# One 512-column matmul for the high and low halves of the features in the FFN up-projection, with the modulation spread over five FFNs

## The chip, the cores and the metric

The kernel runs on one core of one Trainium2 chip. The metric is device time in microseconds. Three runs of the kernel before took 2191.59, 2196.65 and 2203.82 us; the median is 2196.65 us.

## The reference, cut to what matters

Two models run one after the other on a sequence of 256 tokens of width 1024, each with two layers, all in float32. The layers of the first hold a mixer of several attentions and an FFN with a convolution; the layers of the second hold an FFN, a token mixer and a second FFN. That makes six FFNs, numbered here in the order in which they run: FFN 1 and 2 in the layers of the first model, FFN 3 and 4 in the first layer of the second model, FFN 5 and 6 in its last layer.

```python
def conv_glu_ffn(h, w_up, conv_w, conv_b, w_down):          # FFN 1 and 2
    a, u = jnp.split(h @ w_up, 2, axis=-1)                  # w_up: 1024 x 5632
    a = causal depthwise convolution of a, 3 taps, + conv_b
    return (jax.nn.silu(a) * u) @ w_down                    # w_down: 2816 x 1024

def swiglu(h, w13, w2):                                     # FFN 3 to 6
    a, b = jnp.split(h @ w13, 2, axis=-1)
    return (jax.nn.silu(a) * b) @ w2

# second model, layer l
mod = (jax.nn.silu(c) @ ada_w[l] + ada_b[l]).reshape(b_, 3, 3, 1024)
y = swiglu(modulate(x, mod[:, 0, 0], mod[:, 0, 1]), ffn_w13[l, 0], ffn_w2[l, 0])
x = layer_norm(ALPHA * x + 0.5 * (1 + mod[:, 0, 2]) * y, ...)
y = token_mixer(modulate(x, mod[:, 1, 0], mod[:, 1, 1]), ...)
x = layer_norm(ALPHA * x + (1 + mod[:, 1, 2]) * y, ...)
y = swiglu(modulate(x, mod[:, 2, 0], mod[:, 2, 1]), ffn_w13[l, 1], ffn_w2[l, 1])
```

`mod` does not depend on the tokens: it is a product of one vector with a matrix of 1024 by 9216 for each of the two layers.

## The kernel before, in words

**The split.** Each float32 operand of a projection is split into a high part that TensorE multiplies in its fast float32 format and a low part, the rest. A product is the sum of three: high by high, high by low, low by high (`products`, L610 to L612). The weights come in chunks of 1 MB (128 partitions by 2048 numbers) through a ring of three slots. For each chunk ScalarE writes `w_hi` (`hi`, L1101) and VectorE then writes `w_lo` as `raw` minus `w_hi` (`lo`, L1487). A transfer into a slot of `raw` is issued by SyncE once `lo` of the chunk before it in that slot is done.

**An FFN.** It has 22 tiles of 128 hidden features, each with an `a` half and a `u` half, and 33 chunks: 22 for up, 11 for down. TensorE does tile 0, then in turn two up tiles and one down chunk (`turn`), and at the end one up tile and one down chunk. An up tile is 16 steps (8 tiles of the width for each half), and each step is three matmuls that move 256 columns. A down chunk is 24 matmuls that move 512 columns. In FFN 3 to 6 the gate of the residual is spread over the partitions by TensorE behind up tile 0 (`gate_on_all`) and copied by ScalarE (L1305).

**Behind an up tile.** Its result lies in one PSUM bank of two (`UP`). ScalarE waits for the tile and makes the convolution's first tap (L1128) or `silu` (L1131), then `hi` of a later chunk, and, in FFN 1 and 2, `silu` (L1135) behind the other two taps. VectorE makes those two taps (L1514, L1517), `lo` of a later chunk, and then `h` = `silu(a)` times `u` (L1521), still reading PSUM. ScalarE writes `hid_hi` (L1137), VectorE `hid_lo` (L1523). Up tile f+2 waits for `h` of tile f, since it writes the same bank; the down chunk waits for `hid_lo`.

**The modulation.** It is done on VectorE beside the FFNs (`ada`, `modulation`, L1481): 72 chunks of 1 MB from `wm`, two operations for each, 144 in all. Before, FFN 1, 2, 3 and 5 carry 18 chunks each. `silu(c)` comes first (`silu_c`, L1095, on ScalarE) and the first three chunks, six operations, stand on VectorE ahead of `post(0, ...)`; the rest is placed behind `hid_lo` of certain tiles in `turn`.

**Layers.** On every engine a hardware loop (`Fori`) runs over the two layers of each model. At a layer's end PE, ACT and DVE drain, GpSimd clears the semaphores and raises `layer_go`, and all begin the next layer. The order of work on each engine is that of the code, and no planner changes it.

## Time and profile before

| | |
|---|---|
| span of the profiled execution | 2196.9 us |
| its own time | no other than the span is recorded |
| median of three runs | 2196.65 us |
| TensorE matmul busy | 1971.7 us (90%), 13906 matmuls |
| TensorE weight loads busy | 1839.9 us (84%) |
| VectorE busy | 1405.2 us (64%) |
| ScalarE busy | 964.2 us (44%) |
| GpSimd busy | 135.9 us (6%) |
| mean granted TensorE clock | 0.944 |
| moved by DMA | 373.22 MB, mean 170 GB/s |

Matmuls are pipelined, and the duration of one in a row is longer than the distance to the next one's start; the distance is what counts. PE is TensorE, DVE is VectorE, ACT is ScalarE, POOL is GpSimd, SP is SyncE, whose time is that of issuing transfers. The granted clock 1.00 is 2.4 GHz and 0.50 is 1.2 GHz.

### The profile page before, as it was taken

The page shows a single profiled execution, that of the slowest core. Times are in us where ns is not written, and L with a number is a line of the kernel's source. Part 1 is how long each engine was busy: PE and PEld are TensorE (multiplying, and loading weights), DVE is VectorE, ACT ScalarE, POOL GpSimd, SP SyncE. Part 2 cuts the span into 40 slices and gives each one's busy share as a digit, 9 for nine tenths or more (in the row PEclk, how much of TensorE's full clock was granted, in tenths as well). Part 3 has the DMA queues.
Part 4 walks back from the last instruction along what each step waited for, and adds up shares of the span by engine and source line. Part 5 has one row for each costly group of instructions (what it writes and reads, how often), then busy time and mean ns, then how long its engine had stood idle before and what let it go on. Part 6 is the DMA issues. An engine that isn't in the chain of part 4 may idle for free.

```text
span 2196.9 us, 36223 instructions
## 1 busy us (share of the span) xinstructions
PE 1971.7 (90%) x13906; PEld 1839.9 (84%) x13906; DVE 1405.2 (64%) x2155; ACT 964.2 (44%) x1479; POOL 135.9 (6%) x202
## 2 busy tenths in 40 slices
PE   7978999798899969997998979987998898888997
PEld 7868999787899959996888969976997787887996
DVE  4486777448677867667647564556667754756545
ACT  4454444445544444344553334324443545424342
POOL 0000000000000000002005110000000200501000
PEclk9999999989999989998999889997999899988999
DMA  7116676311667667762410235537874251024552
GB/s 270 44 54 267 250 293 246 144 44 58 254 251 293 247 254 273 271 230 83 167 58 1 95 136 178 186 134 267 301 268 176 90 180 39 1 96 140 185 191 77
DMA packets 54109, 373.22 MB, mean 170 GB/s; under 512 B 5984, under 2 KB 6880, under 8 KB 10848
## 3 DMA queue, kind: packets, MB, share of 16 engines
q1 hardware_dynamic: 51392, 361.45, 45.6%
q0 software_dynamic: 2016, 9.07, 1.1%
q8 instruction: 82, 1.34, 0.2%
q10 hardware_dynamic: 576, 0.99, 0.1%
q14 instruction: 43, 0.35, 0.1%
HBM read 370.45 MB, written 1.05 MB: 169 GB/s over the span
## 4 chain that ended last, share of the span: by engine, by line
PE 79%; DVE 13%; ACT 5%; issue 3%; DMA 0%; DVEq 0%; ACTq 0%; POOLq 0%; SPq 0%
PE bank L610 17%; PE bank L611 17%; PE bank L612 17%; PE bank L673 5%; PE bank L674 5%; PE bank L675 5%; PE bank L1030 1%; PE bank L1039 1%; DVE hT_lo L1850 1%; DVE w_lo L1487 1%; PE bank L1038 1%; DVE scratch L1481 1%; PE bank L626 1%; PE bank L649 1%; ACT w_hi L1101 1%
## 5 line engine op out<-in xcount | busy, mean ns | idle before, releaser
L610 PE MATMUL bank<-hT_hi,w_hi 128*128 128x256 f32 x2432 | 703.9, 289 | 56.3 <-DVE hT_lo L1850 29.1
L1487 DVE TENSOR_TENSOR w_lo<-raw,w_hi 128x2048 fp32r<-128x2048 f32 (+2 forms) x270 | 609.0, 2257 | 142.7 <-ACT w_hi L1101 142.3
L611 PE MATMUL bank<-hT_lo,w_hi 128*128 128x256 f32 x2432 | 697.0, 287 | 0.0
L612 PE MATMUL bank<-hT_hi,w_lo 128*128 128x256 f32 x2432 | 696.5, 286 | 0.0
L1101 ACT ACTIVATE w_hi<-raw 128x2048 fp32r<-128x2048 f32 (+2 forms) x270 | 509.0, 1887 | 193.9 <-PE bank L675 119.8
L610 PEld LDWEIGHTS bank<-hT_hi,w_hi 128*128 128x128 f32 x2432 | 473.9, 195 | 66.3 <-DVE hT_lo L1850 31.4
L611 PEld LDWEIGHTS bank<-hT_lo,w_hi 128*128 128x128 f32 x2432 | 473.7, 195 | 4.9 <-issue 2.0
L612 PEld LDWEIGHTS bank<-hT_hi,w_lo 128*128 128x128 f32 x2432 | 473.3, 195 | 0.7
L610 PE MATMUL bank<-w_hi,hT_hi 128*128 128x256 f32 (+2 forms) x800 | 233.0, 291 | 2.0 <-DVE hT_lo L1504 2.0
L611 PE MATMUL bank<-w_lo,hT_hi 128*128 128x256 f32 (+2 forms) x800 | 231.0, 289 | 0.0
L612 PE MATMUL bank<-w_hi,hT_lo 128*128 128x256 f32 (+2 forms) x800 | 230.8, 289 | 0.0
L673 PE MATMUL bank<-w_hi,hid_hi 128*128 128x512 f32 x528 | 207.0, 392 | 8.4 <-DVE hid_lo L1523 8.4
L674 PE MATMUL bank<-w_lo,hid_hi 128*128 128x512 f32 x528 | 206.3, 391 | 0.0
L675 PE MATMUL bank<-w_hi,hid_lo 128*128 128x512 f32 x528 | 205.4, 389 | 0.0
L1481 DVE SCALAR_TENSOR_TENSOR scratch<-scratch 128x1024 f32<-128x1024 f32 x144 | 171.1, 1219 | 12.0 <-ACT scratch L1095 12.0
L610 PEld LDWEIGHTS bank<-w_hi,hT_hi 128*128 128x128 f32 x800 | 159.4, 199 | 4.2 <-issue 4.1
L1131 ACT ACTIVATE scratch<-bank 128x256 f32<-128x256 f32 x88 | 33.8, 384 | 293.9 <-PE bank L612 293.6
L611 PEld LDWEIGHTS bank<-w_lo,hT_hi 128*128 128x128 f32 x800 | 159.4, 199 | 0.0
L612 PEld LDWEIGHTS bank<-w_hi,hT_lo 128*128 128x128 f32 x800 | 159.2, 199 | 0.0
L1523 DVE TENSOR_TENSOR hid_lo<-scratch,hid_hi 128x256 fp32r<-128x256 f32 x132 | 56.2, 425 | 158.5 <-ACT hid_hi L1137 158.5
L673 PEld LDWEIGHTS bank<-w_hi,hid_hi 128*128 128x128 f32 x528 | 99.4, 188 | 29.8 <-DVE hid_lo L1523 11.0
L1521 DVE TENSOR_TENSOR scratch<-scratch,bank 128x256 f32<-128x256 f32 x132 | 55.2, 418 | 107.2 <-ACT scratch L1131 106.2
(352 smaller groups left out, 2375.4 us busy)
## 6 DMA issues: line engine op xcount, KB each, us to landing
raw<-in_wb SPq DMA_DIRECT2D x168, 1024.0 KB, 5.0
raw<-in_wa SPq DMA_DIRECT2D x96, 1024.0 KB, 4.8
scratch<-in_wm SPq DMA_DIRECT2D x72, 1024.0 KB, 6.6
lnw<-in_ln_g POOLq DMA_DIRECT2D x6, 512.0 KB, 4.1
lnw<-in_ln_b POOLq DMA_DIRECT2D x6, 512.0 KB, 5.4
cst<-in_const POOLq DMA_DIRECT2D x1, 2205.0 KB, 9.8
raw<-in_wa SPq DMA_DIRECT2D x4, 512.0 KB, 3.5
scratch<-in_c SPq DMA_DIRECT2D x4, 512.0 KB, 4.3
```

What stands on the lines that cost most here:

```text
L610: nc.tensor.matmul(out, ah, bh, start=(i == 0), stop=False)
L611: nc.tensor.matmul(out, ah, bl, start=False, stop=False)
L612: last = nc.tensor.matmul(out, al, bh, start=False, stop=(i == n - 1))
L673: nc.tensor.matmul(out, ah, bh, start=first and k2 == 0, stop=False, skip_group_check=True)
L674: nc.tensor.matmul(out, ah, bl, start=False, stop=False, skip_group_check=True)
L675: last = nc.tensor.matmul(out, al, bh, start=False, stop=last_one and k2 == 1, skip_group_check=True)
L1101: nc.scalar.activation(w_hi[:, slot, 0:width], raw[:, raw_slot, 0:width], ACT.Copy).then_inc(hi_done, 1)
L1131: nc.scalar.activation(sg[:, f2, :], UP[f2][:, 0:SEQ], ACT.Silu).then_inc(N["sg"], 1)
L1481: return nc.vector.scalar_tensor_tensor(out=w, in0=w, scalar=1.0, in1=cb, op0=ALU.mult, op1=ALU.mult, accum_out=column)
L1487: nc.vector.tensor_tensor(w_lo[:, slot, 0:width], raw[:, raw_slot, 0:width], w_hi[:, slot, 0:width].bitcast(F32), ALU.subtract).then_inc(l ...
L1521: nc.vector.tensor_tensor(h32[:, f2, :], sg[:, f2, :], UP[f2][:, SEQ:2 * SEQ], ALU.mult).then_inc(N["h"], 1)
L1523: nc.vector.tensor_tensor(hid_lo[:, f4, :], h32[:, f2, :], hid_hi[:, f4, :].bitcast(F32), ALU.subtract).then_inc(N["hid_lo"], 1)
```

## The change

The high and low halves of the features become neighbours in one tile `hT`, so that `w_hi` can be multiplied with both in one matmul of 512 columns; `w_lo` is multiplied with the high half and added to the first 256 columns. The columns 256 to 511 hold high by low, the cross product. An up tile now fills two banks, and `UP` takes banks 0 to 3. ScalarE copies the cross products out of both banks (`cross`, 512 numbers for each partition), VectorE adds them to the rest (`whole`, 512 numbers), and everything behind reads `whole` in SBUF. Up tile f+2 waits for that sum and no longer for `h`. On VectorE `lo` of the later chunk now comes right behind the sum, and the modulation's pieces come before `h`, no longer behind `hid_lo`.

The 72 chunks of the modulation are spread over five FFNs: 9, 9, 18, 18 and 18 for FFN 1 to 5. FFN 4 has had none so far. The modulation of layer 1's first half, which FFN 2 used to hold, is now made in FFN 4.

All loops over layers are written out in Python (`for l in range(DEPTH)`), with a drain behind each wait for `layer_go`. The gate's spreading uses banks 4 and 5 for the FFNs, with a wait before the first down chunk.

```diff
+ADA_STAGES = [(0, 0, ADA_N // 2), (0, ADA_N // 2, ADA_N // 2), (0, ADA_N, ADA_N), (1, 0, ADA_N), (1, ADA_N, ADA_N)]
...
-        hT_hi = sb("hT_hi", [P, KT, SEQ], F32R)
-        hT_lo = sb("hT_lo", [P, KT, SEQ], F32R)
+        hT = sb("hT", [P, KT, 2, SEQ], F32R)
+        hT_hi, hT_lo = hT[:, :, 0, :], hT[:, :, 1, :]
...
-        UP, TP, ACC, GATE = ps[0:2], ps[2:6], ps[4:8], ps[2:4]
+        UP, TP, ACC = [psum[:, 2 * k:2 * k + 2, :] for k in range(2)], ps[2:6], ps[4:8]
+        GATE = [ps[4:6], ps[2:4], ps[4:6]]
...
+                if l + 1 < DEPTH:
+                    sp.wait_ge(B["nx"], 2 * TT)
+                load_ffn(lambda j, r: load_b(sp, l, j, B_S0["ffn1"], r), 3 if l + 1 < DEPTH else None)
...
-                        pe.wait_ge(N["h"], f + (h0 - 1))
-                    feature_tile(UP[f2][:, 0:SEQ], slot, 0, features=features)
-                    feature_tile(UP[f2][:, SEQ:2 * SEQ], slot, 1).then_inc(chunk_mm, 1)
+                        pe.wait_ge(N["sum"], f + (h0 - 1))
+                    for half in range(2):
+                        bank = UP[f2][:, half, :]
+                        for k in range(KT):
+                            if features and not half:
+                                pe.wait_ge(features[0]["tp_lo"], features[1] * KT + k + 1)
+                            cols = slice(k * 2 * P + half * P, k * 2 * P + half * P + P)
+                            nc.tensor.matmul(bank, w_hi[:, slot, cols], hT[:, k, :, :].rearrange("p a b -> p (a b)"),
+                                             start=(k == 0), stop=False, skip_group_check=True)
+                            last = nc.tensor.matmul(bank[:, 0:SEQ], w_lo[:, slot, cols], hT_hi[:, k, :],
+                                                    start=False, stop=(k == KT - 1), skip_group_check=True)
+                    last.then_inc(chunk_mm, 1)
...
-            with pe.Fori(0, DEPTH) as l:
+            for l in range(DEPTH):
...
                 pe.wait_ge(layer_go, l + 1)
+                pe.drain()
...
                     act.wait_ge(chunk_mm, pos + (1 + NEW) + split)
+                    nc.scalar.activation(cross[:, f2, :, :], UP[f2][:, :, SEQ:2 * SEQ], ACT.Copy).then_inc(N["cross"], 1)
+                    ahead()
+                    act.wait_ge(N["sum"], f + (h0 + 1))
+                    if not conv:
+                        nc.scalar.activation(sg[:, f2, :], whole[:, f2, 0, :], ACT.Silu).then_inc(N["sg"], 1)
                     if conv:
-                        nc.scalar.activation(cv[:, f2, :], UP[f2][:, 0:SEQ], ACT.Identity, scale=conv_tap(f, 2),
+                        nc.scalar.activation(cv[:, f2, :], whole[:, f2, 0, :], ACT.Identity, scale=conv_tap(f, 2),
                                              bias=conv_tap(f, 3)).then_inc(N["c1"], 1)
-                    else:
-                        nc.scalar.activation(sg[:, f2, :], UP[f2][:, 0:SEQ], ACT.Silu).then_inc(N["sg"], 1)
-                    ahead()
-                    if conv:
                         act.wait_ge(N["cv2"], f + (h0 + 1))
...
+                if l + 1 < DEPTH:
+                    silu_c(3)
...
+                    dve.wait_ge(N["cross"], f + (h0 + 1))
+                    nc.vector.tensor_tensor(whole[:, f2, :, :], UP[f2][:, :, 0:SEQ], cross[:, f2, :, :], ALU.add).then_inc(N["sum"], 1)
+                    ahead()
                     if conv:
...
-                    ahead()
+                    between()
                     dve.wait_ge(N["sg"], f + (h0 + 1))
-                    nc.vector.tensor_tensor(h32[:, f2, :], sg[:, f2, :], UP[f2][:, SEQ:2 * SEQ], ALU.mult).then_inc(N["h"], 1)
+                    nc.vector.tensor_tensor(h32[:, f2, :], sg[:, f2, :], whole[:, f2, 1, :], ALU.mult).then_inc(N["h"], 1)
...
                 lo(split + 1, 1, 1)
-                if part is not None:
-                    dve.wait_ge(c_silu, part + 1)
+                if groups:
+                    dve.wait_ge(c_silu, stage + 1)
                     for k in range(2 * RING):
                         ada(0, k)
                 post(0, 0, 0, lambda: lo(split + 2, 2, 2))
...
+                if groups == 6:
+                    with dve.Fori(0, turns) as j:
+                        turn(j, j + 1, ((0,), (1,), (2,), (3,), (4,), (5,)))
+                elif groups == 3:
+                    with dve.Fori(0, turns // 2) as j:
+                        turn(j * 2, j + 1, ((0,), (1,), (), (2,), (), ()))
+                        turn(j * 2 + 1, j + 1, ((3,), (4,), (), (5,), (), ()))
+                    turn(turns - 1)
```

The order of the instructions shows the change at two places. The first is VectorE's queue at the start of FFN 4, before: the features' low halves, `lo` of chunks 1 and 2, `h` and `hid_lo` of tile 0, then the loop over the turns.

```order
L1845 TENSOR_SCALAR scratch<-bank,modl 128x256
L1850 TENSOR_TENSOR hT_lo<-scratch,hT_hi 128x256 x3
L1486 REGISTER_ALU
L1487 TENSOR_TENSOR w_lo<-raw,w_hi 128x2048 x2
L1521 TENSOR_TENSOR scratch<-scratch,bank 128x256
L1523 TENSOR_TENSOR hid_lo<-scratch,hid_hi 128x256
L1553 UNCONDITIONAL_BRANCH
```

The same place in the changed kernel, where `hT` holds both halves and L1513 is the modulation:

```order
L1896 TENSOR_SCALAR scratch<-bank,modl 128x256
L1901 TENSOR_TENSOR hT<-scratch,hT 128x256 x3
L1519 TENSOR_TENSOR w_lo<-raw,w_hi 128x2048
L1513 SCALAR_TENSOR_TENSOR scratch,moda<-scratch 128x1024 x6
L1556 TENSOR_TENSOR scratch<-bank,scratch 128x512
L1519 TENSOR_TENSOR w_lo<-raw,w_hi 128x2048
L1567 TENSOR_TENSOR scratch<-scratch 128x256
L1569 TENSOR_TENSOR hid_lo<-scratch,hid_hi 128x256
L1594 UNCONDITIONAL_BRANCH
```

Six operations of the modulation and the sum of the cross products now stand between `lo` of chunk 1 and `lo` of chunk 2. The second place is ScalarE's queue at the start of FFN 4, before: the gate's copies, `hi` of chunk 2, `silu` of tile 0 with the table that it needs, `hi` of chunk 3 and `hid_hi`.

```order
L1305 ACTIVATE gateb<-bank 128x512 x2
L1100 REGISTER_ALU
L1101 ACTIVATE w_hi<-raw 128x2048
L1126 REGISTER_ALU
L1131 ACT_TABLE_LOAD
L1131 ACTIVATE scratch<-bank 128x256
L1099 REGISTER_ALU
L1101 ACTIVATE w_hi<-raw 128x2048
L1137 ACTIVATE hid_hi<-scratch 128x256
```

And in the changed kernel:

```order
L1334 ACTIVATE gateb<-bank 128x512 x2
L1122 ACT_TABLE_LOAD
L1122 ACTIVATE scratch<-scratch 128x1024
L1128 ACTIVATE w_hi<-raw 128x2048
L1154 ACTIVATE scratch<-bank 128x512
L1128 ACTIVATE w_hi<-raw 128x2048
L1158 ACTIVATE scratch<-scratch 128x256
L1165 ACTIVATE hid_hi<-scratch 128x256
```

The table load has moved ahead of `hi` of chunk 2, with `silu(c)` behind it, and the copy of the cross products (L1154) stands ahead of `hi` of chunk 3, `silu` of the tile behind it.

## Rows read from the trace of the kernel before

**Rows 1.** The page, chain that ended last, by line.
```profile
PE bank L610 17%; PE bank L611 17%; PE bank L612 17%; PE bank L673 5%; PE bank L674 5%; PE bank L675 5%; PE bank L1030 1%; PE bank L1039 1%; DVE hT_lo L1850 1%; DVE w_lo L1487 1%; PE bank L1038 1%; DVE scratch L1481 1%; PE bank L626 1%; PE bank L649 1%; ACT w_hi L1101 1%
```

**Rows 2.** Windows inside FFN 1, 3, 6: length, busy us of each engine, clock, DMA.
```profile
253.30:270.30 17.00, 17.00 (x123) 16.04 (x122) 13.48 (x17) 8.11 (x9) 0.00 (x0) 1.00 0.53 189
870.40:887.40 17.00, 17.00 (x122) 16.04 (x121) 11.74 (x13) 6.92 (x7) 0.00 (x0) 1.00 0.89 329
2063.90:2080.80 16.90, 16.90 (x122) 15.94 (x121) 8.38 (x7) 6.90 (x7) 0.00 (x0) 1.00 0.54 186
```

**Rows 3.** Timeline, TensorE, FFN 3: start, us, engine, line, operation, tiles, shape.
```profile
871.82 0.39 PE L673 MATMUL bank<-w_hi,hid_hi 128*128 128x512 f32 x1
...
875.90 0.28 PE L610 MATMUL bank<-hT_hi,w_hi 128*128 128x256 f32 x1
```

**Rows 4.** Timeline, TensorE, FFN 2, clock 1.00.
```profile
602.08 0.28 PE L610 MATMUL bank<-hT_hi,w_hi 128*128 128x256 f32 x1
...
604.96 0.28 PE L610 MATMUL bank<-hT_hi,w_hi 128*128 128x256 f32 x1
```

**Rows 5.** Timeline, TensorE, FFN 2, just before, clock 0.50.
```profile
600.01 0.41 PE L612 MATMUL bank<-hT_hi,w_lo 128*128 128x256 f32 x1
...
600.65 0.41 PE L612 MATMUL bank<-hT_hi,w_lo 128*128 128x256 f32 x1
```

**Rows 6.** The page, costliest groups: count, busy us and mean ns, idle before.
```profile
L1487 DVE TENSOR_TENSOR w_lo<-raw,w_hi 128x2048 fp32r<-128x2048 f32 (+2 forms) x270 | 609.0, 2257 | 142.7 <-ACT w_hi L1101 142.3
L1481 DVE SCALAR_TENSOR_TENSOR scratch<-scratch 128x1024 f32<-128x1024 f32 x144 | 171.1, 1219 | 12.0 <-ACT scratch L1095 12.0
L1521 DVE TENSOR_TENSOR scratch<-scratch,bank 128x256 f32<-128x256 f32 x132 | 55.2, 418 | 107.2 <-ACT scratch L1131 106.2
```

**Rows 7.** Timeline, ScalarE, FFN 4, the gate's second copy.
```profile
1291.70 0.60 ACT L1305 ACTIVATE gateb<-bank 128x512 f32<-128x512 f32 x1 [0.26 <-PE bank L649]
```

**Rows 8.** Timeline, ScalarE and VectorE, FFN 1, behind an up tile.
```profile
253.72 0.56 ACT L1128 ACTIVATE scratch<-bank,spa 128x256 f32<-128x256 f32 x1 [0.89 <-PE bank L612]
258.57 0.43 DVE L1523 TENSOR_TENSOR hid_lo<-scratch,hid_hi 128x256 fp32r<-128x256 f32 x1 [0.49 <-ACT hid_hi L1137]
```

**Rows 9.** Waits of TensorE, whole span: us in total, times, longest.
```profile
PE bank L610 <- DVE scratch L1521: 18.5, 4, 7.1
PE bank L673 <- DVE hid_lo L1523: 8.4, 6, 2.1
```

**Rows 10.** Timeline, VectorE, start of FFN 3.
```profile
808.89 2.28 DVE L1487 TENSOR_TENSOR w_lo<-raw,w_hi 128x2048 fp32r<-128x2048 f32 x1
811.10 0.41 DVE L1521 TENSOR_TENSOR scratch<-scratch,bank 128x256 f32<-128x256 f32 x1
```

**Rows 11.** Timeline, ScalarE, start of FFN 3: `silu(c)`.
```profile
799.51 1.28 ACT L1095 ACT_TABLE_LOAD   x1
800.80 1.06 ACT L1095 ACTIVATE scratch<-scratch 128x1024 f32<-128x1024 f32 x1
```

**Rows 12.** Windows behind the starts of FFN 3, 4 and 5, as in rows 2.
```profile
811.70:819.50 7.80, 7.80 (x49) 7.80 (x50) 5.59 (x5) 2.88 (x4) 0.00 (x0) 0.71 0.94 361
1296.00:1303.00 7.00, 7.00 (x60) 7.00 (x60) 5.33 (x7) 4.40 (x5) 0.00 (x0) 1.00 0.59 190
1516.80:1525.20 8.40, 8.40 (x48) 8.40 (x49) 5.59 (x5) 2.92 (x4) 0.00 (x0) 0.64 0.95 365
```

**Rows 13.** Timeline, FFN 1 to layer 1 of the first model.
```profile
394.00 0.20 ACT L1109 ACTIVATE st<-st 128x2 f32<-128x2 f32 x1
397.85 0.17 DVE L1493 RECIPROCAL st<-st 128x2 f32<-128x2 f32 x1 [5.07 <-issue]
```

**Rows 14.** Timeline, FFN 2 to the second model.
```profile
779.93 0.20 ACT L1109 ACTIVATE st<-st 128x2 f32<-128x2 f32 x1
780.80 0.17 DVE L1493 RECIPROCAL st<-st 128x2 f32<-128x2 f32 x1 [2.08 <-POOLq L561]
```

**Rows 15.** Timeline, VectorE, FFN 4 to layer 1 of the second model.
```profile
1488.47 0.18 DVE L1948 COPY modl<-mod 128x36 f32 x1 [4.61 <-issue]
```

More of the change, by code:

```diff
@@ L81 @@
 ADA_N = MOD2 // 2
-ADA_T = ADA_N // RING
+ADA_STAGES = [(0, 0, ADA_N // 2), (0, ADA_N // 2, ADA_N // 2), (0, ADA_N, ADA_N), (1, 0, ADA_N), (1, ADA_N, ADA_N)]
+ADA_AT = [sum(n for _, _, n in ADA_STAGES[:k]) for k in range(len(ADA_STAGES))]
+assert all(n % RING == 0 for _, _, n in ADA_STAGES)
 A_N0 = {"win": 0, "cmp": A_WIN, "wout": A_WIN + A_CMP}
@@ L547, in _ @@
             pool.dma_start(lnw[:, 0, :], t["final_g"].partition_broadcast(P)).then_inc(start_in, 16)
-            with pool.Fori(0, DEPTH) as l:
+            for l in range(DEPTH):
                 for v in (rw, kbd, vr, pc):
@@ L560, in _ @@
                 pool.sem_clear(layer_done)
-                pool.sem_clear(numbers(A))
+                pool.sem_clear(numbers(ONLY_A))
+                pool.sem_clear(numbers(F))
                 pool.sem_inc(layer_go, 1)
-            with pool.Fori(0, DEPTH) as l:
+            for l in range(DEPTH):
                 for sub in range(3):
@@ L695, in ffn @@
                 down(FT - 2, 0, FFN_N - 1, (FFN_N - 1) % RING, last_one=True)
[L697 removed]
+            for l in range(DEPTH):
                 split = l * A_S
@@ L837, in _ @@
                 pe.wait_ge(layer_go, l + 1)
+                pe.drain()
             pe.wait_ge(start_in, 32)
             pe.wait_ge(FIN["x"], TT)
-            with pe.Fori(0, DEPTH) as l:
+            for l in range(DEPTH):
                 split = l * B_N + S_A
@@ L1164, in _ @@
             root_mean_square(NEXT, 0)
-            with act.Fori(0, DEPTH) as l:
+            for l in range(DEPTH):
                 split = l * A_S
@@ L1313, in _ @@
             act.wait_ge(FIN["x"], TT)
-            with act.Fori(0, DEPTH) as l:
+            for l in range(DEPTH):
                 split = l * B_N + S_A
@@ L1552, in ffn @@
                 post(0, 0, 0, lambda: lo(split + 2, 2, 2))
-                with dve.Fori(0, (FT - 2) // 4) as j:
-                    turn(j)
+                if groups == 6:
[6 more added lines that the diff above has]
+                    turn(turns - 1)
+                else:
+                    with dve.Fori(0, turns) as j:
+                        turn(j)
                 post(FT - 1, 1, 1, (lambda: lo(split + FFN_N, 0, 0)) if more else (lambda: None))
-            with dve.Fori(0, DEPTH) as l:
+            for l in range(DEPTH):
                 split = l * A_S
@@ L1861, in _ @@
             dve.wait_ge(FIN["x"], TT)
-            with dve.Fori(0, DEPTH) as l:
+            for l in range(DEPTH):
                 split = l * B_N + S_A
```

159 lines of the change are left out of this document (91 added, 68 removed).

## The prediction

> **What bounds the kernel now.** I read the chain of work that ended last first: 66% of the span is TensorE in six lines, the three matmuls of an up step (L610 to L612, 17% each) and the three of a down step (5% each) [rows 1]. Not all of the first three is FFN work, since the mixers' projections use the same lines; 2112 of their steps are up steps (six FFNs, 22 tiles, 16 steps). Then windows inside single FFNs: TensorE is busy through all 17 us at clock 1.00 in FFN 1, 3 and 6, while VectorE has 13.5, 11.7 and 8.4 us of work and ScalarE 8.1 to 6.9 [rows 2]. So inside an FFN the distance from matmul to matmul sets the time, and other engines count only where TensorE waits for them. By the table of waits that is at the start of the four FFNs that carry modulation (18.5 us in 4 waits) and at each FFN's last down chunk (8.4 us in 6) [rows 9]. Two places outside belong to the change as well: the ends of layers [rows 13 to 15].
>
> **Distance of matmuls.** Eighteen matmuls of 512 columns take from 871.82 to 875.90: 227 ns each [rows 3]. Twenty-four of 256 columns take from 602.08 to 604.96: 120 ns each [rows 4]. At 2.4 GHz the columns alone are 213 and 107 ns, so each matmul pays about 13 ns beyond its columns, whatever its width. At 1.2 GHz three take 0.64 us, 213 ns each, which is the columns alone [rows 5]. The change keeps the columns of a step (768) and drops one matmul of three: 360 ns become 227 + 120 = 347. No row shows a 256-column matmul with new weights right behind a 512-column one. Its bounds are 107 ns (weights fully ready behind the long one: 26 ns saved per step) and 133 ns (the 13 ns are still paid: nothing saved). I take 120, since both widths show the same 13 ns. Saved: 2112 x 13 ns = 27.5 us.
>
> The Trainium skill ("TensorE: Matmul & The Clock Gate", section "Wait — 56ns, not 53.3ns?") puts the fixed cost of a warm matmul at about 2.5 ns and at nothing when cold. By that figure the term would be 2112 x 2.5 ns = 5.3 us. The cold half agrees with this trace (213 ns), the warm one does not (13 ns).
>
> **Steady turns.** Added per up tile: a copy of 512 numbers out of PSUM on ScalarE, 0.60 us like the gate's copy [rows 7], and a sum of 512 on VectorE. For that no row of this shape stands: 256 numbers take 0.42, and between 256 and 2048 a number costs (2257 - 418) / 1792 = 1.03 ns [rows 6], so 0.68 us (bounds: 0.42 for half the size, 0.84 for two such operations). VectorE's work in two tiles and a down chunk becomes: FFN 1 and 2 13.5 + 1.4 - 1.8 (half the modulation has left) = 13.1 us, FFN 3 and 5 13.1, FFN 4 8.4 + 1.4 + 3 x 1.2 = 13.4, all within the new period of 17.0 - 0.42 = 16.6. Latency is closer. In FFN 1 an up tile ended at 253.3 and its `hid_lo` at 259.0, 5.7 us later [rows 2, 8]; the down chunk behind the next tile needs it 5.8 + 2.7 = 8.5 us later. In the changed order the sum (0.6) and one modulation piece (1.2) come into that path: 7.5 against 5.55 + 2.7 = 8.3. `lo` for the tile behind the down chunk comes after all of this on VectorE and then has about 0.5 us to spare; in FFN 3 to 5, without the taps, about 1.5. So I count no wait in steady turns, and if that cover is gone each 0.4 us in a pair of tiles eats its whole gain.
>
> **Starts.** TensorE waits for tile 0 before it may write tile 2. In FFN 3 the six modulation operations ended at 808.9, then `lo` of chunk 2 and `h` released it [rows 10]. Now the sum comes first and `lo` last: about 0.2 us later, and tiles 0 and 1 are done 0.4 earlier, so the wait is 0.6 longer (FFN 3 and 5: +1.2 in all). In FFN 1 and 2 the two taps leave the path and the wait shrinks by 0.4, but what was put off (taps, `hid_lo` of tiles 0 and 1, `lo` of chunks 3 to 5) then comes late once for the next chunks; I work this out as 1.7 us of small waits, +1.3 each, +2.6. FFN 6: the sum is in front of `lo` of chunk 2, +0.9.
>
> FFN 4 is the costly one. It gets the modulation's head for the first time. The gate's copies end at 1292.3 [rows 7]; the table load and `silu(c)` take 2.3 us (the table had to be loaded here before too, but behind `hi`) [rows 11]; the six operations take 7.0 (from the end of `silu(c)`, 801.9, to 808.9 in FFN 3 [rows 10, 11]); sum and `lo` 2.9: 1304.5. TensorE's tile 1 starts once the gate's matmuls are done, about 1291.5, and ends 5.5 us later at 1297.0, where it ran on without a wait so far [rows 12]. A wait of 7.5 us, as long as those of FFN 3 and 5 (up to 7.1 [rows 9]). Behind those the granted clock was 0.71 over 7.8 us and 0.64 over 8.4 us [rows 12]: 2.3 and 3.0 us lost. I take 2.6 for FFN 4. Its start costs +10.1. Starts together: 1.2 + 2.6 + 0.9 + 10.1 = +14.8 us.
>
> **Ends.** The last down chunk waits for `hid_lo` of tile 21. Copy and sum come into that path: 0.60 + 0.68 + 0.15 for the hand-over = +1.4 in FFN 1, 2, 4, 6. In FFN 3 and 5 `lo` of the next chunk (2.3 us) now also stands behind the sum; so far it ran while ScalarE was at work: +2.0. Together +9.6. Bounds: 0.7 and 2.5 for each.
>
> **Ends of layers.** From ScalarE's last operation to VectorE's next one it takes 397.85 - 394.20 = 3.65 us where the layer loop goes back [rows 13], and 780.80 - 780.13 = 0.67 where the code goes straight on [rows 14], with the same drain and hand-over by GpSimd. Written out, the first model's boundary gives 3.0 us. In the second model VectorE's idle time before layer 1 is 4.61 us with nothing released in it [rows 15]; I leave 0.9 of it: 3.7. Together -6.7. What is next there are TensorE's transposes, which wait for VectorE anyway. Bounds: 0 (the added drains or the longer program take it) and 9.
>
> The Trainium skill ("Runtime: NRT & Kernel Launch", section "Instruction fetch mechanics") says that instructions are fetched strictly forward and that a taken branch out of the small window forces a fetch. The idle times at the two loop-backs agree with it. The same rule would speak against the longer bodies of the turn loops, which stay; no window in an FFN before shows such idle time.
>
> **Clock.** Longer waits at the ends may bring low clock into what follows. In FFN 1 to 6 that could cost up to 1.7 us each; I take 1.5 in all. The rest of the edits (where the modulation's bias is added, banks for the gate, fewer transfers in FFN 1 and 2) lies beside other work and I count it at nothing; in FFN 4 the transfers come on top of the weights, as they do in FFN 3, where they are hidden.
>
> **The sum.** -27.5 + 14.8 + 9.6 - 6.7 + 1.5 = -8.3 us. The profiled execution has 2196.9 us, 0.25 above the median of the runs, so its time can be used as it is: 2188.6, told as 2189 us. That is 0.38% less. A measurement of this kernel tells about 0.5% (11 us) from no change.
>
> **Rivals.**
> 1. The chain through copy and sum becomes the bound (slower). For it: half a microsecond of spare time in FFN 1 and 2, worked out from durations only. Against it: 3 us of free VectorE time per pair. It decides once the chain is more than 0.5 us longer than I have it in FFN 1 and 2, and 1.5 us in FFN 3 to 5. If it eats the gain of the 50 pairs in FFN 1 to 5, 50 x 0.42 = 21 us: 2210 us.
> 2. The 13 ns are paid again behind a 512-column matmul, or come with something else than the matmul. For it: no row has this pair. Then 27.5 us of the sum are gone: 2216 us. The skill's 2.5 ns would leave 2211.
> 3. Weights are ready behind the long matmul and the short one takes 107 ns. Against it: the 512-column matmuls have ready weights too, and pay 13 ns. Another 27 us: 2162 us.
> 4. The layers' ends give nothing, since the change adds a drain and a longer program. 2195 us.
> 5. The waits at starts and ends are smaller than worked out, since a part of the clock loss of FFN 4 and of the ends doesn't come: 2181 us.
>
> **How the numbers follow.** Forecast 0.55 (its own range 2181 to 2197), rival 1 0.09, rival 2 0.05, rival 3 0.08, rival 4 0.17, rival 5 0.06. Faster by over 0.5% is below 2185.7: 0.20 of the forecast's 0.55, rivals 3 and 5: 0.34. Slower is above 2207.6: rivals 1 and 2: 0.14. The rest, 0.52, is within. The range reaches from 2172 to 2209: most of rivals 4 and 5 and the edge of 1 lie in it.
>
> **What would show it.** Distances of 227 and 120 ns in up steps, and 16.56 us from one down chunk to the next in place of 16.98, with TensorE busy throughout. A new wait of 7 to 8 us in FFN 4 on VectorE's `w_lo`, and low clock behind it. Waits at the last down chunk near 3 to 4 us. VectorE's first operation of layer 1 within 1 us of the drain, in both models. It is wrong if periods in FFN 1 or 2 stay near 17 us, if the pair of matmuls takes 360 ns, or if FFN 4 starts without the wait.

## The result and the profile after

| | before | changed |
|---|---|---|
| median, same chip | 2196.24 us (2191.59 to 2203.82, 10 runs) | 2203.66 us (2197.97 to 2208.69, 10 runs) |
| ratio to before | 1 | 1.0031 [1.0016, 1.0046] |
| span of the profiled execution | 2196.9 us | 2201.2 us |
| mean granted clock | 0.944 | 0.935 |
| TensorE matmuls | 13906 | 11794 |
| VectorE, ScalarE busy | 1405.2, 964.2 us | 1486.4, 1043.7 us |

The changed kernel is 0.31% slower, 6.8 us. 0.38% less was forecast. The time lies inside the range of 2172 to 2209, the forecast's sign is wrong. The changed kernel measured again (`e11` below) has the same ratio.

The page of the changed kernel has the chain by line first, to be read against [rows 1], and the costliest groups, against [rows 6]; L679 is the 512-column matmul, L681 the 256-column one, L1556 the sum and L1154 the copy of the cross products.

```profile
PE bank L679 21%; PE bank L681 11%; PE bank L624 6%; PE bank L625 6%; PE bank L626 6%; PE bank L698 5%; PE bank L700 5%; PE bank L699 5%; DVE w_lo L1519 2%; DVE hT L1901 2%; DVE scratch L1513 2%; PE bank L1056 1%; PE bank L1065 1%; PE bank L1064 1%; PE bank L640 1%
...
L679 PE MATMUL bank<-hT,w_hi 128*128 128x512 f32 x2112 | 765.1, 405 | 39.6 <-DVE w_lo L1519 24.0
...
L1556 DVE TENSOR_TENSOR scratch<-bank,scratch 128x512 f32<-128x512 f32 x132 | 91.4, 692 | 209.1 <-ACT scratch L1154 207.5
...
L1154 ACT ACTIVATE scratch<-bank 128x512 f32<-128x512 f32 x132 | 78.4, 594 | 235.0 <-PE bank L681 235.0
```

The bound has not changed: TensorE in the up and down steps. The two added operations cost 0.692 and 0.594 us (0.68 and 0.60 were taken). Windows inside FFN 1 and FFN 3, as in [rows 2]:

```profile
260.30:277.10 16.80, 16.80 (x90) 14.32 (x89) 13.07 (x18) 9.14 (x11) 0.00 (x0) 1.00 0.69 252
870.40:887.20 16.80, 16.80 (x91) 14.32 (x90) 12.94 (x15) 8.17 (x10) 0.00 (x0) 1.00 0.96 374
```

TensorE is busy throughout at full clock, VectorE has 13.1 and 12.9 us of work where 13.1 was forecast. No other engine holds it up, and still the period is not the forecast one. The first matmuls of two down chunks, eight periods apart, before and changed:

```profile
836.48 0.40 PE L673 MATMUL bank<-w_hi,hid_hi 128*128 128x512 f32 x1
...
972.31 0.40 PE L673 MATMUL bank<-w_hi,hid_hi 128*128 128x512 f32 x1
```
```profile
837.13 0.40 PE L698 MATMUL bank<-w_hi,hid_hi 128*128 128x512 f32 x1
...
971.48 0.40 PE L698 MATMUL bank<-w_hi,hid_hi 128*128 128x512 f32 x1
```

A period is the time from one down chunk's first matmul to the next one's. 135.83 / 8 = 16.98 us became 134.35 / 8 = 16.79; forecast were 16.56. The same 16.79 stands in all six FFNs. It is 0.19 us / 32 = 6 ns per step instead of 13. The steps themselves, to be compared with [rows 3] and [rows 4]:

```profile
269.77 0.28 PE L681 MATMUL bank<-hT,w_lo 128*128 128x256 f32 x1
269.89 0.40 PE L679 MATMUL bank<-hT,w_hi 128*128 128x512 f32 x1
270.13 0.28 PE L681 MATMUL bank<-hT,w_lo 128*128 128x256 f32 x1
270.25 0.40 PE L679 MATMUL bank<-hT,w_hi 128*128 128x512 f32 x1
270.49 0.28 PE L681 MATMUL bank<-hT,w_lo 128*128 128x256 f32 x1
```

From L679 to L681 are 0.24 us, and from L681 to L679 0.12: over the 80 pairs from 260 to 300 us the means are 236 and 117 ns, 353 in all.

The waits of TensorE, against [rows 9]:

```profile
PE bank L679 <- DVE w_lo L1519: 24.0, 6, 7.3
PE bank L698 <- DVE hid_lo L1569: 18.4, 8, 3.5
```

Both have grown, the first from 18.5 to 24.0 (at the starts, 21.9 of it in FFN 3, 4 and 5), the second from 8.4 to 18.4 (at the ends, but for 0.8 in the first turns of FFN 1 and 2). At FFN 4 the forecast wait is there. VectorE does the last of the head's six operations (the head is what of the modulation stands ahead of tile 0), the sum, `lo`, and `h`. TensorE's last matmul of tile 1 starts at 1298.13, its next one at 1305.72, 7.59 us later:

```profile
1301.63 1.22 DVE L1513 SCALAR_TENSOR_TENSOR scratch<-scratch 128x1024 f32<-128x1024 f32 x1
...
1302.78 0.69 DVE L1556 TENSOR_TENSOR scratch<-bank,scratch 128x512 f32<-128x512 f32 x1
1303.38 2.28 DVE L1519 TENSOR_TENSOR w_lo<-raw,w_hi 128x2048 fp32r<-128x2048 f32 x1
1305.58 0.42 DVE L1567 TENSOR_TENSOR scratch<-scratch 128x256 f32<-128x256 f32 x1
```

At an FFN's end the last down chunk does six matmuls, waits for `hid_lo` of tile 21 and does the other 18. In FFN 1:

```profile
384.01 0.39 PE L700 MATMUL bank<-w_hi,hid_lo 128*128 128x512 f32 x1
...
387.92 0.79 PE L698 MATMUL bank<-w_hi,hid_hi 128*128 128x512 f32 x1 [3.52 <-DVE hid_lo L1569]
```

A wait at an end is told here and below as the distance of these two starts less 0.23 us, which is 3.7 (the profile's own idle time, 3.52, starts at the modelled end of the first). The windows of the last 18 matmuls of FFN 1 to 6, behind that wait; in the kernel before these 18 took 4.0 us in every FFN.

```profile
387.92:393.70 5.78, 5.72 (x18) 4.30 (x18) 1.31 (x3) 2.14 (x4) 0.00 (x0) 0.75 0.00 0
771.13:778.00 6.87, 6.87 (x18) 5.12 (x18) 1.34 (x3) 2.14 (x4) 0.00 (x0) 0.61 0.00 0
987.60:993.70 6.10, 6.00 (x18) 4.45 (x18) 5.51 (x13) 0.82 (x1) 0.00 (x0) 0.72 0.38 153
1478.50:1484.60 6.10, 6.00 (x18) 4.43 (x18) 3.75 (x7) 0.81 (x1) 0.00 (x0) 0.72 0.00 0
1697.70:1703.80 6.10, 5.98 (x18) 4.45 (x18) 5.44 (x13) 0.79 (x1) 0.00 (x0) 0.72 0.40 158
2183.40:2190.00 6.60, 4.38 (x18) 3.30 (x18) 4.76 (x8) 0.83 (x1) 0.00 (x0) 1.00 0.00 0
```

The waits ahead of them are 3.67, 3.67, 3.63, 2.00, 3.63 and 2.00 us (before: 2.28, 2.28, 1.81, 0.61, 1.81, 0.61). Five of six runs of 18 stand at low clock for a part. From first to last start they take 5.33, 6.49, 5.61, 5.60, 5.59 and 3.99 us: 8.5 us more than before. In a second profiled execution of the changed kernel (`e11`) the waits are the same, FFN 4's 18 ran at full clock, and it is 7.0 us.

Ends of layers, against [rows 13] and [rows 15]: ScalarE's last and VectorE's next operation at the end of FFN 1, and VectorE's first for layer 1 of the second model.

```profile
396.18 0.20 ACT L1136 ACTIVATE st<-st 128x2 f32<-128x2 f32 x1
...
397.01 0.17 DVE L1525 RECIPROCAL st<-st 128x2 f32<-128x2 f32 x1 [2.05 <-POOLq L574]
...
1494.54 0.18 DVE L1999 COPY modl<-mod 128x36 f32<-128x36 f32 x1 [0.81 <-POOLq L608]
```

From the end of ScalarE's operation (396.38) 3.65 us became 0.63, and 4.61 us idle became 0.81: both as forecast.

### The profile page after: what moved, and what is told of

Same layout as the page of the kernel before. It is cut to its first block, busy times and chain, and to the rows that moved or that the text cites. A ratio compares the mean times of both kernels' runs of the same rounds, so it can differ in the third digit from the quotient of the medians.

```text
span 2201.2 us, 30627 instructions
## 1 busy us (share of the span) xinstructions
PE 1973.6 (90%) x11794; PEld 1734.5 (79%) x11794; DVE 1486.4 (68%) x2287; ACT 1043.7 (47%) x1612; POOL 136.7 (6%) x202
## 4 chain that ended last, share of the span: by engine, by line
PE 78%; DVE 14%; ACT 5%; issue 2%; DMA 0%; DVEq 0%; ACTq 0%; POOLq 0%; SPq 0%
PE bank L679 21%; PE bank L681 11%; PE bank L624 6%; PE bank L625 6%; PE bank L626 6%; PE bank L698 5%; PE bank L700 5%; PE bank L699 5%; DVE w_lo L1519 2%; DVE hT L1901 2%; DVE scratch L1513 2%; PE bank L1056 1%; PE bank L1065 1%; PE bank L1064 1%; PE bank L640 1%
## 5 line engine op out<-in xcount | busy, mean ns | idle before, releaser
L679 PE MATMUL bank<-hT,w_hi 128*128 128x512 f32 x2112 | 765.1, 405 | 39.6 <-DVE w_lo L1519 24.0
L681 PE MATMUL bank<-hT,w_lo 128*128 128x256 f32 x2112 | 598.3, 283 | 0.0
L679 PEld LDWEIGHTS bank<-hT,w_hi 128*128 128x128 f32 x2112 | 403.8, 191 | 143.8 <-DVE w_lo L1519 26.6
L681 PEld LDWEIGHTS bank<-hT,w_lo 128*128 128x128 f32 x2112 | 405.7, 192 | 3.2 <-issue 1.0
L624 PE MATMUL bank<-w_hi,hT 128*128 128x256 f32 (+2 forms) x800 | 232.7, 291 | 1.9 <-DVE hT L1536 1.9
L1556 DVE TENSOR_TENSOR scratch<-bank,scratch 128x512 f32<-128x512 f32 x132 | 91.4, 692 | 209.1 <-ACT scratch L1154 207.5
L626 PE MATMUL bank<-w_hi,hT 128*128 128x256 f32 (+2 forms) x800 | 230.8, 288 | 0.0
L625 PE MATMUL bank<-w_lo,hT 128*128 128x256 f32 (+2 forms) x800 | 230.7, 288 | 0.0
L698 PE MATMUL bank<-w_hi,hid_hi 128*128 128x512 f32 x528 | 212.0, 401 | 18.4 <-DVE hid_lo L1569 18.4
L1154 ACT ACTIVATE scratch<-bank 128x512 f32<-128x512 f32 x132 | 78.4, 594 | 235.0 <-PE bank L681 235.0
L1513 DVE SCALAR_TENSOR_TENSOR scratch<-scratch 128x1024 f32<-128x1024 f32 x144 | 173.7, 1219 | 18.3 <-ACT scratch L1122 18.3
L624 PEld LDWEIGHTS bank<-w_hi,hT 128*128 128x128 f32 x800 | 159.1, 199 | 4.0 <-DVE hT L1536 2.7
L625 PEld LDWEIGHTS bank<-w_lo,hT 128*128 128x128 f32 x800 | 159.1, 199 | 0.0
L626 PEld LDWEIGHTS bank<-w_hi,hT 128*128 128x128 f32 x800 | 158.8, 199 | 0.0
L700 PEld LDWEIGHTS bank<-w_hi,hid_lo 128*128 128x128 f32 x528 | 100.9, 191 | 23.4
L699 PEld LDWEIGHTS bank<-w_lo,hid_hi 128*128 128x128 f32 x528 | 101.4, 192 | 19.6
```

Of the source, the lines that this page charges most:

```text
L624: nc.tensor.matmul(out, ah, bh, start=(i == 0), stop=False)
L625: nc.tensor.matmul(out, ah, bl, start=False, stop=False)
L626: last = nc.tensor.matmul(out, al, bh, start=False, stop=(i == n - 1))
L679: nc.tensor.matmul(bank, w_hi[:, slot, cols], hT[:, k, :, :].rearrange("p a b -> p (a b)"), start=(k == 0), stop=False, skip_group_check=True)
L681: last = nc.tensor.matmul(bank[:, 0:SEQ], w_lo[:, slot, cols], hT_hi[:, k, :], start=False, stop=(k == KT - 1), skip_group_check=True)
L698: nc.tensor.matmul(out, ah, bh, start=first and k2 == 0, stop=False, skip_group_check=True)
```

## The experiments

Ratios are to the kernel before, in runs on the same chip. The changed kernel stands at 1.0031 in this measure. Where two kernels are compared by us, it is the difference of their ratios times 2197 us; each ratio is uncertain by 3 to 5 us.

**Layers alone (`e1`).** The kernel before with its loops over layers written out and the added drains, nothing else.

```diff
-            with dve.Fori(0, DEPTH) as l:
+            for l in range(DEPTH):
...
                 dve.wait_ge(layer_go, l + 1)
+                dve.drain()
```

> The kernel before with only the loops over layers written out (and the drains). Theory A (the loop-back at a layer's end costs 3.0 us in the first model and 3.7 in the second, all of it given back): 2196 - 6.7 = about 2189.5 us, VectorE's idle time of 5.1 and 4.6 us at the two layer ends shrinks to about 2 and 1, and the rest of the trace is as before. Rival: what is next (transfers, TensorE's own start) is as late, then 2196 us within 2.

Measured: 2193.1 us, ratio 0.9975 [0.9957, 0.9993]: 5.5 us less (1.5 to 9.5 by the interval), where 6.7 were forecast. In its trace ScalarE's last operation of the first model's layer ends at 395.32 and VectorE's next starts at 395.89, 0.57 us, and VectorE's idle time ahead of the second model's layer 1 is 0.75. The term holds within that interval.

**Blocks (`e2`).** In each half of an up tile first the eight 512-column matmuls, then the eight 256-column ones.

```diff
-                            last = nc.tensor.matmul(bank[:, 0:SEQ], w_lo[:, slot, cols], hT_hi[:, k, :],
+                        for k in range(KT):
+                            last = nc.tensor.matmul(bank[:, 0:SEQ], w_lo[:, slot, cols_of(half, k)], hT_hi[:, k, :],
                                                     start=False, stop=(k == KT - 1), skip_group_check=True)
```

> The changed kernel with another order of the matmuls in each half of an up tile: first the eight of 512 columns, then the eight of 256. The period of a pair of tiles with its down chunk was 16.98 us before and is 16.79 in the changed kernel, where 16.56 had been forecast, and in its trace the distance behind a 512-column matmul is about 235 ns in up steps and 227 in down chunks. Theory (the alternation costs: a 512-column matmul among 256-column ones takes 8 ns more): the period falls to about 16.6 us, some 54 times 0.2 = 11 us less than the changed kernel, about 2192. Rival (the wide matmul on the features costs 233 to 235 ns wherever it stands): period 16.79 and 2203 us as before.

Measured: ratio 1.0010 [0.9993, 1.0027]. Two first matmuls of down chunks, eight periods apart:

```profile
837.34 0.40 PE L699 MATMUL bank<-w_hi,hid_hi 128*128 128x512 f32 x1
...
970.25 0.40 PE L699 MATMUL bank<-w_hi,hid_hi 128*128 128x512 f32 x1
```

132.91 / 8 = 16.61 us, the forecast's 16.56 but for 0.05. So a matmul left out does save 12 of the forecast's 13 ns, and the interleaving took 6 of them back. Only 4.6 of the 11 us show in the ratio. The 18 matmuls at the ends took 6.8 us in FFN 1 and 2, 6.7 and 6.5 in FFN 3 and 5, and 5.6 in FFN 4 and 6, together 5.4 us more than in the changed kernel, about what the ratio misses. FFN 3 and FFN 1:

```profile
986.25:993.40 7.15, 7.04 (x18) 5.23 (x18) 5.70 (x13) 0.83 (x1) 0.00 (x0) 0.60 0.33 132
385.20:392.50 7.30, 7.21 (x18) 5.34 (x18) 1.34 (x3) 2.14 (x4) 0.00 (x0) 0.58 0.00 0
```

**A plain last tile (`e3`).** The changed kernel; only tile 21 of each FFN is made in three matmuls of 256 columns, without copy and sum.

```diff
-                up(FT - 1, 1, FFN_N - 2, (FFN_N - 2) % RING)
+                up(FT - 1, 1, FFN_N - 2, (FFN_N - 2) % RING, plain=True)
```

> The changed kernel with the last up tile of each FFN done in the old way: three matmuls of 256 columns, no copy, no sum, ScalarE and VectorE read PSUM. Theory (the longer path behind the last tile costs its wait and low clock behind it): the six waits at the last down chunk fall from 3.7 (2.0 in FFN 4 and 6) to 1.8 to 2.3 (0.6), 9.3 us in all, and the 18 matmuls behind them take 4.4 us in place of 5.7 to 6.9 in five FFNs, 8.6 us in all: 2203.7 - 18 = 2186 us. Rival (the low clock there comes from elsewhere, by chance of the phase): only the waits go, 2194 us.

Measured: 2190.1 us, ratio 0.9964 [0.9950, 0.9977], 14.7 us less than the changed kernel, between theory (18) and rival (9). Six tiles of 132 decide the sign. The waits at the ends are those of the kernel before again (2.27, 2.28, 1.81, 0.61, 1.81, 0.61), and five of six runs of 18 take 4.0 us at full clock, where the rival had the low clock stay (FFN 2's take 5.6). These are the windows of FFN 1 and FFN 3:

```profile
383.85:389.75 5.90, 4.22 (x18) 3.30 (x18) 2.13 (x4) 3.31 (x6) 0.00 (x0) 1.00 0.00 0
974.50:980.60 6.10, 4.45 (x19) 3.30 (x18) 4.67 (x12) 2.54 (x3) 0.00 (x0) 1.00 0.49 169
```

**Without the modulation in FFN 4 (`e4`).** The 18 chunks of FFN 4 are left out, so layer 1's first modulation is not computed.

```diff
-                load_ffn(lambda j, r: load_b(sp, l, j, B_S0["ffn1"], r), 3 if l + 1 < DEPTH else None)
+                load_ffn(lambda j, r: load_b(sp, l, j, B_S0["ffn1"], r), None)
```

> The changed kernel without the 18 modulation chunks of FFN 4: they are left out altogether, with silu(c) there, and layer 1's first half of the modulation is wrong for it. Theory (the head of six operations makes TensorE wait 7.5 us in FFN 4 and brings low clock): the wait falls to about 0.5 us as in FFN 6, 9 to 10 us less than the changed kernel, 2194 us. Rival (the low clock stays, since it starts in the mixer's end): 7 us less, 2197. If VectorE's modulation pieces also delay steady turns there, the period in FFN 4 falls below 16.79, which neither expects.

Measured: 2198.24 us, ratio 0.9995 [0.9979, 1.0011], 7.9 us less than the changed kernel, which by the intervals is neither told from the theory's 9 to 10 nor from the rival's 7. The trace has both in part. The wait of 7.59 us is gone, and the low clock behind it too: 1.00 from 1287.2 us to the first down chunk, where the changed kernel had 0.77 from 1305.7 to 1312.8, 1.6 us lost (2.6 were forecast). Low clock in tile 0, ahead of that wait, is there in both. From the end of FFN 3 to the first down chunk of FFN 4 it takes 313.4 us in `e4`, against 312.3 before and 319.6 in the changed kernel's profiled execution (322.4 in its second one: the mixer between them has low clock of its own that differs by 3 us from execution to execution).

**Both together (`e5`).** Blocks and plain last tile.

> The changed kernel with both edits tried singly so far: in each half of an up tile first the eight 512-column matmuls, then the eight 256-column ones, and the last up tile of each FFN in three matmuls of 256 columns as before. Theory A (a 512-column matmul costs 8 ns more only where it alternates with 256-column ones, and the low clock at the FFNs' ends comes from the 3.7 us waits there): periods of 16.61 us, waits at the ends of 2.3, 1.8 and 0.6 us with full clock behind them. The last tile alone gave a ratio of 0.9964 to the kernel before; 0.18 us in 10 pairs of tiles in 6 FFNs is 10.8 us more: 0.9915. Rival B (what the blocks win, the clock takes back wherever it can: alone they gave only 4.7 of 10.8 us): low clock again at the ends, about 0.9943.

Measured: 2183.09 us, ratio 0.9928 [0.9912, 0.9945], between the two. Periods are 16.61 us. Low clock came behind the 2.3 us waits of FFN 1 and FFN 2 (none in the kernel before), here FFN 1, and not behind the shorter ones:

```profile
378.60:384.70 6.10, 5.97 (x18) 4.47 (x18) 1.35 (x3) 2.16 (x4) 0.00 (x0) 0.72 0.00 0
```

Each costs 1.6 us, and the plain last tile alone had it in FFN 2 only. The one in FFN 1 accounts for a part of the 2.9 us by which the ratio misses theory A's 0.9915; rival B holds for two ends of six.

**The head spread out.** `e7_no_head` is the changed kernel with no modulation ahead of tile 0; `e6_combined` has blocks and the plain last tile as well. `ada_slots` gives one or two pieces to each chunk of the turns, and `silu(c)` moves behind tile 0's `post` on ScalarE. With it VectorE's loop over the turns of these FFNs is written out, and the transfers of the modulation are issued in step with the pieces.

```diff
                 lo(split + 1, 1, 1)
+                post(0, 0, 0, lambda: lo(split + 2, 2, 2))
                 if groups:
                     dve.wait_ge(c_silu, stage + 1)
-                    for k in range(2 * RING):
-                        ada(0, k)
-                post(0, 0, 0, lambda: lo(split + 2, 2, 2))
...
+                    for j in range(turns):
+                        turn(j, 0, ada_slots(groups)[6 * j:6 * j + 6])
...
-                silu_c(l)
...
+                if stage is not None:
+                    silu_c(stage)
```

> The changed kernel with nothing but the modulation's head spread over the turns (no six operations ahead of tile 0, silu(c) behind it). It keeps the alternating matmuls and the sum of the cross products in every tile. Theory A: the three waits of 7.6 us at the starts go, with 2.3 to 3 us of low clock each, the ends stay (3.7 and 2.0 us, low clock behind them): about 26 us below the changed kernel, a ratio of 0.991 to the kernel before. Rival C (pieces make the turns late, since here sum, taps and pieces share VectorE): periods above 16.79 in FFN 3 to 5, a ratio above 0.997. Rival D (clock lost at the starts is lost later instead): waits gone, but 5 us or more of the gain missing, with more low clock inside the FFNs.

> Blocks and a plain last tile as in the run before this one, and the modulation without its head: VectorE does none of the six operations ahead of tile 0; all 18 or 36 pieces of an FFN lie in the turns, two or one beside each chunk, silu(c) comes behind tile 0 on ScalarE, and each transfer of the modulation is issued one ring later in step with them. Theory A (the 7.6 us waits at the start of FFN 3, 4 and 5 are the head's, and the low clock behind them is theirs): no wait there, 7.6 us and 2.3 to 3 us of clock less in each, about 28 us together, less 2 for what is put off: ratio about 0.980 (2155 us where before takes 2199). Rival C (the pieces are only moved: two of them in a down chunk's slot make `lo` of the next chunk late in FFN 3 to 5, or a transfer comes late): waits of TensorE on `w_lo` inside turns, less than half of the gain, 0.986 or more.

Measured: e7 2178.5 us, 0.9894 [0.9877, 0.9911]; e6 2155.09 us, 0.9795 [0.9778, 0.9812]. Theory A's 0.991 and 0.980 are met. Periods stay at 16.79 and 16.61 but for the first of an FFN (up to 16.90 and 16.81), so rival C did not come. In e7's trace, from one FFN's last down matmul to the next one's first, it takes 33.8 us ahead of FFN 3 in place of 42.8, 315.7 ahead of FFN 4 in place of 319.6, and 39.3 ahead of FFN 5 in place of 46.3. Of TensorE's waits for `w_lo` in up steps, 24.0 us in the changed kernel, the second row is left in e6; the first is the ends' wait, as in the kernel before:

```profile
PE bank L719 <- DVE hid_lo L1598: 8.4, 6, 2.1
...
PE bank L698 <- DVE w_lo L1544: 1.2, 4, 0.3
```

**One width (`e8`).** The second matmul of a step is 512 columns wide too and adds the product low by low.

> The changed kernel with the second matmul of an up step also 512 columns wide (low weights by both halves; the product low by low is added, which the reference's precision doesn't need). All matmuls of an up tile then have one width, while high and low weights still alternate. Theory A (the 8 ns come from the two widths alternating): 227 ns each, 454 per step, period 16.79 + 32 x 0.100 = 20.0 us, span about 2201 + 2112 x 0.100 = 2412 us. Rival E (they come from alternating high and low weights or from a 512-column moving operand out of `hT`): 235 ns each, 470 per step, period 20.5, span about 2446 us.

Measured: 2402.7 us (one run).

```profile
903.14 0.39 PE L698 MATMUL bank<-w_hi,hid_hi 128*128 128x512 f32 x1
...
1062.71 0.39 PE L698 MATMUL bank<-w_hi,hid_hi 128*128 128x512 f32 x1
```

159.57 / 8 = 19.95 us, 453 ns per step, 226 to 227 for each matmul. High and low weights alternate here as well, and nothing is paid for it. Rival E falls.

**In twos (`e12`).** Two matmuls of 512 columns, then their two of 256.

> The changed kernel with the steps of an up tile taken in twos: two matmuls of 512 columns, then their two of 256. Half as many changes of width. Theory A (each change from one width to the other and back costs 8 ns): 4 ns per step in place of 8, period 16.79 - 32 x 0.004 = 16.66 us. Rival H (the cost hangs on the mix within a longer stretch, not on the neighbour): 16.79. Rival I (one neighbour of the same width is enough for all of it): 16.60.

Measured: 2199.36 us (one run), with low clock behind five of six waits at the ends.

```profile
834.98 0.39 PE L700 MATMUL bank<-w_hi,hid_hi 128*128 128x512 f32 x1
...
967.67 0.40 PE L700 MATMUL bank<-w_hi,hid_hi 128*128 128x512 f32 x1
```

132.69 / 8 = 16.59 us. My theory A of 4 ns for each change of width (16.66) falls, rival I holds: one neighbour of the same width is enough, and the cost comes only where widths alternate at every matmul. Why is open: no row shows what the engine does in those 6 ns.

**The end in another order (`e9`, with `e10` and `e11` beside it).** `e9` is as e6, and tile 21 is made before the down chunk of tiles 18 and 19. `e10` is e9 with the old three matmuls in every up tile, and `e11` is the changed kernel again.

```diff
+                        if last and r == 1:
+                            up(FT - 1, 1, pos + 2, 0, plain=True)
+                            down(f, 2 * r, pos + 3, 1)
+                        else:
                             down(f, 2 * r, pos + 2, 0, first=first and r == 0)
```

> The combined version (blocks, plain last tile, no head) with the last two chunks' order changed: tile 21 comes before the down chunk of tiles 18 and 19, so that this chunk (5.45 us) and the first quarter of the last one (1.36) cover the 5.7 us from the end of tile 21 to its `hid_lo`. Theory A (the waits at the ends are only this path, and the low clock behind them is theirs): no wait at the last down chunk, 9.4 us less in six FFNs, and 1.6 us of clock less in FFN 1 and 2; from 0.9795 to a ratio of about 0.974. Rival F (the end only passes its lateness on, to `lo` of the chunk behind the FFN or to the residual): less than 4 us, 0.978 or more.

> The same as the run before this one, with every up tile in three matmuls of 256 columns per step, as in the kernel before: no cross products' copy and sum, up tile f+2 waits for `h`. It shows what the 512-column matmul is worth once blocks, starts and ends are in order. Theory A: period 16.98 in place of 16.61 us, with 10.5 pairs in six FFNs 23 us more: a ratio of 0.984. Rival G (the wider matmul's gain is lost elsewhere, by clock or by the longer path behind a tile): 0.979 or less.

> The changed kernel once more, unaltered, beside the two runs before this one. Expected a ratio of 1.003 to the kernel before, between 1.001 and 1.005, waits of 3.7 and 2.0 us at the ends with low clock behind most of them.

Measured: e9 2144.41 us, ratio 0.9757 [0.9734, 0.9780]; e10 2161.04 us, 0.9832 [0.9807, 0.9857]; the changed kernel again 2204.77 us, 1.0031 [1.0015, 1.0048]. In e9 no wait for `hid_lo` is left, and from the first to the last down matmul the six FFNs take 13.5 us less than in e6 (996.5 and 1009.9), near theory A's 12.6. The ratio shows 8.3 of them, halfway between theory and rival F. The two profiled executions can't say where the rest went: e9's had more low clock over the span, 247 us against 211, but e6's was the fastest of its five runs (2148.37 us, median 2155.09). With an interval of 5 us to each side the rest can't be settled. Theory A's 0.984 for e10 is met, and rival G's 0.979 or less lies outside the interval. e10 against e9 says what the wider matmul brings where its neighbours and its ends are in order: 16.5 us (23 were forecast by its periods of 16.98 against 16.61; the FFNs' down-to-down stretches differ by 19.1).

**A late end with the old matmuls (`e13`).** The kernel before, with two spare products on VectorE ahead of `h` of tile 21; their results are not used.

```diff
+                    for k in range(extra):
+                        nc.vector.tensor_tensor(spare[:, k, :], UP[f2][:, :], cst[:, 0:512], ALU.mult)
                     nc.vector.tensor_tensor(h32[:, f2, :], sg[:, f2, :], UP[f2][:, SEQ:2 * SEQ], ALU.mult).then_inc(N["h"], 1)
```

> The kernel before, with its three 256-column matmuls, and two spare products of 512 numbers on VectorE ahead of `h` of each FFN's last tile (their results are not used). They take 0.69 us each by the changed kernel's sum, so `hid_lo` of tile 21 comes 1.3 to 1.4 us later, as in the changed kernel, and nothing else is different. Theory A (the wait's length brings the low clock at the FFNs' ends, whatever matmuls stand ahead of it): waits of 3.6 us in FFN 1 and 2, 3.1 in FFN 3 and 5, 1.9 to 2.0 in FFN 4 and 6, low clock behind most of the first four, 8 us of wait and 6 to 9 of clock: a ratio of 1.006 to 1.008. Rival J (the matmuls of 512 columns in the up tiles bring it): waits as told with full clock behind them, 1.003 to 1.004.

Measured: 2207.35 us, ratio 1.0037 [1.0018, 1.0055]. The size is rival J's, the cause is theory A's. In FFN 3 and 5 the spare products lay beside ScalarE's `hi`, which `hid_hi` waits for anyway, and the wait stayed at 1.81 us. FFN 4 and 6 got 1.81 (full clock behind it) and FFN 1 and 2 3.47, with low clock behind it in both:

```profile
390.88:396.80 5.92, 5.83 (x18) 4.43 (x18) 1.43 (x4) 2.24 (x4) 0.00 (x0) 0.71 0.00 0
783.60:789.70 6.10, 5.85 (x18) 4.45 (x18) 1.58 (x4) 2.39 (x4) 0.00 (x0) 0.72 0.00 0
```

4 x 1.2 us of wait and 2 x 1.6 of clock are 8.0 us, and 8.1 were measured by the ratio. The profiled execution itself was the longest of nine (2212.89 us); what it has beyond that lies ahead of FFN 1 and between FFN 1 and 2 (2.7 and 4.1 us more than before). There is no matmul of 512 columns in an up tile here: the longer wait was enough at both ends that had it.

All profiled executions of this case together, by the wait at the last down chunk and whether any of the 18 matmuls behind it ran at low clock:

| wait | ends | with low clock | kernels |
|---|---|---|---|
| none | 12 | 0 | e9, e10 |
| 0.6 us | 10 | 0 | before, e1, e3, e5, e6 |
| 1.8 us | 14 | 0 | the same, e13 |
| 2.0 us | 14 | 6 | changed (twice), e2, e4, e7, e8, e12 |
| 2.3 us | 10 | 6 | before 0 of 2, e1 1, e3 1, e5 2, e6 2 |
| 3.5 to 3.7 us | 30 | 29 | changed (twice), e2, e4, e7, e8, e12, e13 |

## Why the prediction was wrong

By its own terms, in us; the measured column is from the profiled executions before and changed, but for the layers, which are e1's ratio.

| term | forecast | measured |
|---|---|---|
| 2112 steps | -27.5 | -12.5 (6 ns each) |
| starts of FFN 1, 2, 3, 5, 6 | +4.7 | -1 (-1.4 and -0.7 in two executions) |
| start of FFN 4 | +10.1 | +7.3 (10.1 in the second execution, 7.9 by e4's ratio) |
| waits at the ends | +9.6 | +9.2 |
| clock at the ends | +1.5 (all clock) | +8.5 (7.0 in the second execution) |
| ends of layers | -6.7 | -5.5 |
| sum | -8.3 | +6.0; span +4.3, ratio +6.8 |

The span's +4.3 divides into +9.0 inside the six FFNs (first to last down matmul), +7.3 from FFN 3 to FFN 4, -4.7 and -5.9 in the two stretches with a layer's end, and -1.5 elsewhere. These stretches hold the mixers with their own low clock, so they don't give single terms.

**The step that failed** is "360 ns become 227 + 120 = 347". Durations of the two widths were each read in stretches of their own width, and both were right there (e2 and e8 have them again). The mix was named as not shown by any row, its bounds 107 and 133 ns for the short matmul were right too (it came to 126 by the sum), but 120 was taken "since both widths show the same 13 ns", as if the cost belonged to a matmul and not to its neighbourhood. Rival 2, the 13 ns paid again, came about by half: 15.0 us of the term are gone. The Trainium skill's figure ("TensorE: Matmul & The Clock Gate", section "Wait — 56ns, not 53.3ns?") would have made the term 5.3 us. The interleaved result of 12.5 us lies nearer to that 5.3 than to the forecast's 27.5, but not for its reason: in blocks 0.37 us / 32 = 12 ns per step are saved, about this case's 13 ns for each matmul. What the runs show in place of the step is 353 ns for a pair that alternates one by one and 348 where each width has a neighbour of its own.

**The second term that was mis-sized** is the clock at the ends: 1.5 us for 8.5. The waits themselves were forecast to 0.4 us. That a wait half again as long could change what the clock does was mentioned ("up to 1.7 us each") and then taken at 1.5 in all; neither figure was worked out from a row. 1.4 us of added wait in FFN 1 and 2 carried 1.3 and 2.5 us of clock behind them. By e3 the six last tiles cost 14.7 us in all, more than everything the interleaved steps save.

These two misses are 22.0 us, more than the 15.1 between forecast and ratio. The starts took up to 8.5 us less than forecast and hid a part of them. That was luck: FFN 4's wait came as forecast and its stretch was 2.8 us below the forecast in one execution and on it in the other, and for the rest no mechanism had been named. The time fell into the stated range because misses of either sign partly cancelled.

**What was right.** No wait in steady turns (rival 1 did not come), the durations of copy and sum, VectorE's load, FFN 4's wait (7.59 us for 7.5), the ends' waits, the layers within e1's interval (rival 4's sign, nothing gained, lies outside it). The waits of FFN 3 and 5 grew by 0.3 us each (7.33 to 7.59) where 0.6 were forecast. The starts of FFN 1 and 2 were forecast 1.3 us later each; their wait for tile 0 fell from 2.4 and 2.6 to 0.9 and 1.4 us, more than the first turn's small waits of 0.9 to 1.0 us took back. FFN 6, forecast 0.9 later, took 32.9 us from its transposes to its first down matmul in place of 32.4.

The best version measured is e9: 0.9757 of the kernel before, with every idea of the change in it (one 512-column matmul, `whole` in SBUF, modulation over five FFNs). Of its 60.2 us below the changed kernel (ratios, 0.0274 x 2197), 14.7 are by e3 alone the last tile and 30.1 by e7 alone the modulation's head, if the gains add up; blocks and the reordered end are the rest.
